# First attention's squares as rounded high and low parts, and two later norm sums one feature tile earlier

## The chip, the core and the metric

The kernel runs on one core of a Trainium2 chip. The metric is the device time of one execution in microseconds (us), as the median of several runs. TensorE (PE) multiplies matrices into PSUM; VectorE (DVE), ScalarE (ACT) and GpSimd (POOL) do the elementwise work; SyncE (SP) issues nearly all loads. Each engine has a queue of its own that it works through in order; they meet only at semaphores.

## The reference, cut to what matters

Two transformer blocks run one after the other on a sequence of 512 positions of width 1024, in float32. The first block has a sliding-window attention whose queries (8 heads of 64) and keys (2 heads of 64) are normalised head by head:

```python
def rmsnorm(x, gain):
    xf = x.astype(jnp.float32)
    y = xf * lax.rsqrt(jnp.mean(xf * xf, axis=-1, keepdims=True) + NORM_EPS)
    return (y * gain.astype(jnp.float32)).astype(x.dtype)
...
    q = rmsnorm(q.reshape(B, S, N_Q_HEADS, HEAD_DIM), q_gain)
    k = rmsnorm(k.reshape(B, S, N_KV_HEADS, HEAD_DIM), k_gain)
...
        x = x + merged @ w_out[l]
        x = x + conv_gated_mlp(rmsnorm(x, ffn_norm[l]), w_up[l], conv_w[l], conv_b[l], w_down[l])
```

The means over 64 features are the sums that the first part of the change makes in another way. The second part moves the sums of two norms over the whole width of 1024: the one ahead of the gated MLP (called norm 2 in the kernel) and the one with which the second block begins (norm 3).

## The kernel before

Features lie on the 128 partitions and positions along the free dimension, so a projection is a set of products of a 128x128 weight tile with a 128x512 activation tile. To keep float32 accuracy each operand is split in a rounded high part and the rounded rest (type fp32r), and three passes are made for each feature tile: high by high, high by low, low by high (lines 394 to 396). The weights come in strips of 128x1024, loaded by SP. For each strip n DVE makes `w_high` (`make_high`, line 368) and POOL makes `w_low` (`make_low`, line 373). A strip's two parts live in rings of four (`w_high`, `w_low`), the raw strip in a ring of two (`w_raw`), so the load of strip n + 2 waits for `make_low` of strip n, and `make_high` of strip n + 4 waits until PE has used strip n.

The part that matters here is the projection of keys, values and queries, strips 8 to 13 (`N_QKV` + m, m = 0 to 5): keys m = 0, values m = 1, queries m = 2 to 5. PE runs the six strips in turn, cut in two pieces each from m = 1 on (`cuts`), and puts small work between the pieces. Between the pieces of strip m = 2 to 5 stands `qkv_sum(m - 2)`, and `qkv_sum(4)` follows after the first of four small mixing products (`mix(0)`, line 1017). The five sums j = 0 to 4 belong to the keys and the four query strips. For each j the chain is:

- ACT squares the finished projection out of PSUM into `sq` (line 1757).
- PE multiplies `sq` by the constant `blocks`, which holds ones in two 64x64 blocks, so that each partition gets its head's sum (`qkv_sum`, line 955). Both are plain float32, and the profile has two PE instructions for one such product.
- ACT takes Ln and Exp (lines 1747 and 1750), DVE multiplies the projection by the result (`i1_norm`, line 2292).

ACT does them in turn: squares j, Ln j, Exp j, squares j + 1. DVE has other work between the norms, in a fixed order: norm 0, `make_high` of strips 12 and 13, a copy of the values, two `bias_h` tables (line 2298); norm 1, `make_high` 14; norm 2, two copies of turned tokens, `make_high` 15; norm 3, two copies (line 2305), `make_high` 16; the first mixing result (lines 2327 and 2330), norm 4. POOL only makes `w_low` of strips 12 to 17 in this stretch. After `mix(1)` PE waits for the last Exp and starts the attention scores (`a_scores`, line 1031).

Norm 2 works so: while the output projection ends, ACT writes squares of each new feature tile and POOL adds the first seven up in `root`. PE starts the MLP's up projection on the raw tiles, before they are normalised (`product_two`, lines 407 to 411, six passes for a feature tile, since two strips go together), and stops after three feature tiles to sum over the partitions (`norm_rest`, lines 498 and 500, again plain float32). ACT takes the root, DVE scales (line 529), ACT rounds, DVE makes the low part (line 533), tile by tile; PE's product with strip m = 2 needs these tiles one by one. Norm 3 has the same form ahead of the second block's projections.

Of the kernel before, what the change touches and what calls it, by code (L numbers as in the profile page):

```python
# [7 lines left out]
ACT = mybir.ActivationFunctionType  # L8
ALU = mybir.AluOpType
AX = mybir.AxisListType  # L10
F32 = mybir.dt.float32
# [4 lines left out]
KT = D // P  # L16
S = 512
# [65 lines left out]
def program(nc, x, mix_norm, w_in, q_norm, k_norm, sinks, sgu_norm, w_s, b_s, w_oa, w_ob, w_out,  # L83
# [4 lines left out]
    with ExitStack() as ctx:  # L88
# [24 lines left out]
        sq = sb("sq", [P, 2, L])  # L113
# [111 lines left out]
        ps = ctx.enter_context(nc.psum_tensor("ps", [P, 8, 512], F32))  # L225
# [144 lines left out]
        def make_low(pool, n, i=0):  # L370

            pool.wait_ge(high_made, i + (n + 1))
            pool.tensor_tensor(w_low[:, n % RING, :], w_raw[:, n % RAW, :],  # L373
                               w_high[:, n % RING, :].bitcast(F32), ALU.subtract).then_inc(low_made, 1)
# [24 lines left out]
        def product_two(pe, banks, n, high, low, done, ks=(0, KT), used=None, moving=None):  # L399

            for k in range(*ks):
                mh, ml = (moving or hx)(k)
                at = slice(k * P, (k + 1) * P)
                pe.wait_ge(s[high], done + k + 1)
                for o in range(2):
                    slot = (n + o) % RING
                    pe.matmul(ps[:, banks[o], :], w_high[:, slot, at], mh, start=k == 0, stop=False)  # L407
                    pe.matmul(ps[:, banks[o], :], w_low[:, slot, at], mh, start=False, stop=False)  # L408
                pe.wait_ge(s[low], done + k + 1)
                for o in range(2):  # L410
                    mm = pe.matmul(ps[:, banks[o], :], w_high[:, (n + o) % RING, at], ml, start=False, stop=k == KT - 1)  # L411
                    if k == KT - 1:
                        mm.then_inc(strip_used, 1)
                if used and k < KT - 1:
                    mm.then_inc(s[used], 1)
# [22 lines left out]
        def yx(k):  # L438
# [5 lines left out]
            norm_sq norm_sum norm_added norm_root norm_scaled norm_high norm_low  # L444
            gelu_done sv_sq sv_sum sv_root sv_normed sv_turned sv_tok_ready mixed mix_biased mix_gated
            mix_high
            i1_sq i1_sum i1_ln i1_root i1_normed v_made
            j_staged j_bias a_scored a_masked a_neg a_part a_exp a_sink_exp a_probs a_turned
            a_copied a_summed a_y a_high a_low gate_kept
            g_sig m_part m_whole m_high_ m_low_ o_added  # L450
# [198 lines left out]
        def _(pool):  # L649
# [14 lines left out]
            pool.wait_ge(s["more_in"], 16 * N_EARLY)  # L664
            for dst, src in more[N_EARLY:]:
                pool.dma_start(dst, src).then_inc(s["more_in"], 16)
            for n in range(2, N_GATE):
                make_low(pool, n)
                if n in (9, 10):
                    pool.wait_ge(s["sv_sq"], n - 7)  # L670
                    if n == 10:
                        pool.wait_ge(s["sv_sum"], 1)
                    pool.tensor_tensor(root[:, 1, 0:S], sq[:, 0, 0:S], sq[:, 1, 0:S] if n == 9 else root[:, 1, 0:S],
                                       ALU.add).then_inc(s["sv_sum"], 1)
                if n == 3:

                    pool.wait_ge(s["meta_in"], 16)
                    pool.affine_select(out=ws_raw[:], in_=ws_raw[:], compare_op=ALU.is_ge, fill=0.0, base=0,
                                       pattern=[[0, 8], [-1, P]], channel_multiplier=1).then_inc(s["ws_made"], 1)
            for n0, n1 in ((N_GATE, N_MERGE), (N_MERGE, N_OUT)):  # L680
                with pool.Fori(0, (n1 - n0) // 4) as turn:
                    i = turn * 4
                    for n in range(n0, n0 + 4):
                        make_low(pool, n, i)
# [181 lines left out]
        def _(pe):  # L866
# [82 lines left out]
            bank = [4, 5, 6, 7, 4, 5]  # L949

            def qkv_sum(j):
                pe.wait_ge(s["i1_sq"], j + 1)
                if j >= 2:
                    pe.wait_ge(s["i1_root"], j - 1)
                pe.matmul(ps[:, j % 2, :], blocks[:], sq[:, j % 2, 0:S], start=True, stop=True)\
                    .then_inc(s["i1_sum"], 1)


# [125 lines left out]
            mix(0)  # L1084
            qkv_sum(4)
            mix(1)
            pe.wait_ge(s["i1_root"], 5)
            a_scores(0, 0, first=True)
            mix(2)
            mix(3)  # L1090
# [31 lines left out]
            def raw(k):  # L1122
                return m_high[:, FT - KT + k, :], m_low[:, FT - KT + k, :]

            product_two(pe, (0, 1), N_UP, "raw_high", "raw_low", 0, (0, 3), moving=raw)
            norm_rest(pe, 2, ps[:, 7, :])
            product_two(pe, (0, 1), N_UP, "raw_high", "raw_low", 0, (3, KT), moving=raw)
            for m in range(2, 4):
                pe.wait_ge(low_made, N_UP + m + 1)
                pe.wait_ge(s["o_added"], 8)  # L1130
# [18 lines left out]
                            part == 0, part == 2, ready=("z_low", 8 * part) if m == 0 else None)\  # L1149
                        .then_inc(strip_used, 1)  # L1150
            pe.wait_ge(low_made, N_LAT + 2)
            product_two(pe, (0, 1), N_LAT, "raw_high", "raw_low", KT, (0, 3), "raw_used")
            norm_rest(pe, 3, ps[:, 6, :])
            product_two(pe, (0, 1), N_LAT, "raw_high", "raw_low", KT, (3, KT), "raw_used")

            def kv_rows(m, k0, k1):
                pe.wait_ge(low_made, N_LAT + m + 1)
# [520 lines left out]
        def _(act):  # L1678
# [62 lines left out]
            def i1_root(j):  # L1741
                act.wait_ge(s["i1_sum"], j + 1)
                if j >= 2:
                    act.wait_ge(s["i1_normed"], j - 1)
                if j == 1:
                    act.wait_ge(s["sv_normed"], 4)
                act.activation(root[:, j % 2, 0:S], ps[:, j % 2, :], ACT.Ln, bias=eps[:, 0:1], scale=1.0 / HD)\
                    .then_inc(s["i1_ln"], 1)
                act.wait_ge(s["i1_ln"], j + 1)
                act.activation(root[:, j % 2, 0:S], root[:, j % 2, 0:S], ACT.Exp, scale=-0.5)\  # L1750
                    .then_inc(s["i1_root"], 1)

            for j in range(5):
                act.wait_ge(strip_used, N_QKV + strips[j] + 1)
                if j >= 2:
                    act.wait_ge(s["i1_sum"], j - 1)
                act.activation(sq[:, j % 2, 0:S], ps[:, banks[j], :], ACT.Square).then_inc(s["i1_sq"], 1)
                if j == 0:
                    act.wait_ge(strip_used, N_QKV + 2)
                    act.activation(v_f[:], ps[:, 5, :], ACT.Copy).then_inc(s["v_made"], 1)  # L1760
                if j < 4:
                    i1_root(j)
# [39 lines left out]
            a_pair(3, more=False)  # L1802


            act.activation(blocks_r[:], blocks[:], ACT.Copy)
            act.activation(ones_r[:], ones[:], ACT.Copy)
            after(act, "att")
            with act.Fori(0, 2) as i:
# [422 lines left out]
        def _(dve):  # L2231
# [54 lines left out]
            dve.wait_ge(s["more_in"], 16 * N_MORE)  # L2286

            def i1_norm(j):
                dve.wait_ge(s["i1_root"], j + 1)
                dst = k_t[:] if j == 0 else q_t[:, j - 1, :]  # L2290
                gain = col(V_AK) if j == 0 else aq_gain[:, 0:1]
                dve.scalar_tensor_tensor(dst, ps[:, [4, 6, 7, 4, 5][j], :], gain, root[:, j % 2, 0:S],
                                         ALU.mult, ALU.mult).then_inc(s["i1_normed"], 1)
# [673 lines left out]
```

## Time and profile before

| | us |
|---|---|
| median of 3 runs | 1268.66 |
| lowest and highest run | 1268.24, 1270.27 |
| the profiled execution | 1269.92 |
| its span in the trace | 1268.2 |
| PE busy with matmuls | 1246.8 |
| DVE busy | 720.4 |
| POOL busy | 637.5 |
| ACT busy | 467.8 |

The span reaches from the first to the last instruction in the trace; the profiled execution's own time is 1.7 us longer. The busy times overlap: an engine that has less to do than PE still matters where PE waits for it. Line numbers are those of the kernel before, where nothing else is said.

### The profile page before, as it was taken

How to read it: one execution, taken by the hardware profiler on the slowest of the kernel's cores; microseconds unless marked ns; L12 is line 12 of the kernel's file. 1: busy time of each engine (PE TensorE's matmuls, PEld its weight loads, DVE VectorE, ACT ScalarE, POOL GpSimd, SP SyncE). 2: the span in 40 equal slices, each digit the busy share in tenths (PEclk: the TensorE clock that was granted, in tenths of full speed). 3: DMA queues.
4: the chain of work that ended last, by engine and by line, in shares of the span. 5: the costliest groups of instructions: out<-in, count | busy, mean ns of one | idle time of the engine just before them, and what ended most of it. 6: DMA issues, size and time to landing. Idle time of an engine off the chain costs nothing.

```text
span 1268.2 us, 19971 instructions
## 1 busy us (share of the span) xinstructions
PE 1246.8 (98%) x6772; PEld 1031.6 (81%) x6772; DVE 720.4 (57%) x1380; ACT 467.8 (37%) x1019; POOL 637.5 (50%) x426
## 2 busy tenths in 40 slices
PE   7999999999999999999999999999999999999998
PEld 6877777877788888888887878988988888888876
DVE  5236655566865545452223788888744566666640
ACT  4233333412322222221112476776511445555531
POOL 5443333237353444445664154544537877777722
PEclk9999999999999999999999999999999999999999
DMA  7322222223233333323334211211134333322113
GB/s 206 101 67 67 83 83 67 68 83 101 87 111 99 92 90 91 107 79 92 91 97 124 67 51 40 59 36 38 55 82 112 92 86 81 83 79 79 66 34 100
DMA packets 190612, 105.42 MB, mean 83 GB/s; under 512 B 19175, under 2 KB 186445, under 8 KB 190557
## 3 DMA queue, kind: packets, MB, share of 16 engines
q1 hardware_dynamic: 189748, 102.82, 28.7%
q10 hardware_dynamic: 376, 1.18, 0.2%
q0 software_dynamic: 432, 0.69, 0.2%
q8 instruction: 33, 0.54, 0.2%
q14 instruction: 23, 0.18, 0.0%
HBM read 102.57 MB, written 2.10 MB: 83 GB/s over the span
## 4 chain that ended last, share of the span: by engine, by line
PE 87%; DVE 4%; ACT 3%; issue 2%; POOL 2%; DMA 1%; ACTq 0%; DVEq 0%; SPq 0%; POOLq 0%
PE ps L394 20%; PE ps L395 19%; PE ps L396 19%; PE ps L425 8%; PE ps L1572 1%; PE ps L1574 1%; PE ps L1573 1%; PE ps L1230 1%; PE ps L1489 1%; PE ps L1521 1%; POOL w_low L373 1%; PE ps L1501 1%; PE ps L407 1%; PE ps L408 1%; PE ps L411 1%
## 5 line engine op out<-in xcount | busy, mean ns | idle before, releaser
L373 POOL TENSOR_TENSOR w_low<-w_raw,w_high 128x1024 fp32r<-128x1024 f32 x180 | 440.6, 2450 | 435.5 <-DVE w_high L368 430.3
L394 PE MATMUL ps<-h_high,w_high 128*128 128x512 f32 x810 | 325.7, 402 | 0.5 <-DVE h_low L533 0.4
L395 PE MATMUL ps<-h_low,w_high 128*128 128x512 f32 x810 | 320.2, 395 | 0.0
L396 PE MATMUL ps<-h_high,w_low 128*128 128x512 f32 x810 | 318.8, 394 | 0.0
L368 DVE CAST w_high<-w_raw 128x1024 fp32r<-128x1024 f32 x183 | 144.0, 789 | 116.9 <-DMA w_raw<-in_w_in_dram 39.4
L394 PEld LDWEIGHTS ps<-h_high,w_high 128*128 128x128 f32 x810 | 152.2, 188 | 36.0 <-issue 2.3
L396 PEld LDWEIGHTS ps<-h_high,w_low 128*128 128x128 f32 x810 | 152.4, 188 | 34.7
L395 PEld LDWEIGHTS ps<-h_low,w_high 128*128 128x128 f32 x810 | 152.2, 188 | 32.2 <-issue 1.0
L1839 ACT ACTIVATE z<-ps,cv 128x512 f32<-128x512 f32 x42 | 32.7, 778 | 148.3 <-PE ps L396 148.3
L2470 DVE SCALAR_TENSOR_TENSOR z<-ps,cv,z 128x511 f32<-128x511 f32 x42 | 31.5, 749 | 92.9 <-ACT z L1839 92.8
L396 PE MATMUL ps<-m_high,w_low 128*128 128x512 f32 x176 | 69.4, 395 | 0.0
L395 PE MATMUL ps<-m_low,w_high 128*128 128x512 f32 x176 | 69.4, 395 | 0.0
L394 PE MATMUL ps<-m_high,w_high 128*128 128x512 f32 x176 | 69.4, 394 | 0.0
L425 PE MATMUL ps<-h_high,w_high 128*128 128x264 f32 x304 | 65.1, 295 | 0.0
L425 PE MATMUL ps<-h_high,w_low 128*128 128x264 f32 x304 | 61.8, 285 | 0.0
L425 PE MATMUL ps<-h_low,w_high 128*128 128x264 f32 x304 | 61.7, 284 | 0.0
L792 POOL TENSOR_TENSOR nb<-rel,mask 128x128 f32<-128x128 f32 (+1 forms) x96 | 53.4, 595 | 0.3 <-DMA rel<-in_rel_bias_dram 0.3
L2778 DVE TENSOR_SCALAR ne<-ne,nm 128x272 f32<-128x272 f32 (+2 forms) x64 | 51.3, 842 | 1.1
L425 PEld LDWEIGHTS ps<-h_high,w_high 128*128 128x128 f32 x304 | 47.8, 189 | 3.9 <-issue 2.8
L425 PEld LDWEIGHTS ps<-h_low,w_high 128*128 128x128 f32 x304 | 47.1, 188 | 0.0
L425 PEld LDWEIGHTS ps<-h_high,w_low 128*128 128x128 f32 x304 | 47.0, 188 | 0.0
L1858 ACT ACTIVATE x_t<-z 128x512 f32<-128x512 f32 x8 | 9.8, 1224 | 100.5 <-DVE z L2498 100.5
(406 smaller groups left out, 2424.4 us busy)
## 6 DMA issues: line engine op xcount, KB each, us to landing
w_raw<-in_w_in_dram SPq DMA_DIRECT2D x150, 256.0 KB, 3.2
w_raw<-in_w_up_dram SPq DMA_DIRECT2D x88, 256.0 KB, 3.2
w_raw<-in_w_out_dram SPq DMA_DIRECT2D x44, 256.0 KB, 3.0
w_raw<-in_w_down_dram SPq DMA_DIRECT2D x32, 256.0 KB, 3.0
w_raw<-in_w_down_dram SPq DMA_DIRECT2D x16, 192.0 KB, 2.6
rel<-in_rel_bias_dram SPq DMA_DIRECT2D x16, 192.0 KB, 3.7
w_raw<-in_w_ob_dram SPq DMA_DIRECT2D x8, 256.0 KB, 3.0
w_raw<-in_w_oa_dram SPq DMA_DIRECT2D x8, 256.0 KB, 4.1
```

The costliest lines, as they stand in the source:

```text
L368: dve.tensor_copy(w_high[:, n % RING, :], w_raw[:, n % RAW, :]).then_inc(high_made, 1)
L373: pool.tensor_tensor(w_low[:, n % RING, :], w_raw[:, n % RAW, :], w_high[:, n % RING, :].bitcast(F32), ALU.subtract).then_inc(low_made, 1)
L394: pe.matmul(acc, wh, mh, start=first and k == 0, stop=False)
L395: pe.matmul(acc, wh, ml, start=False, stop=False)
L396: done = pe.matmul(acc, wl, mh, start=False, stop=last and k == tiles - 1)
L407: pe.matmul(ps[:, banks[o], :], w_high[:, slot, at], mh, start=k == 0, stop=False)
L408: pe.matmul(ps[:, banks[o], :], w_low[:, slot, at], mh, start=False, stop=False)
L425: done = pe.matmul(ps[:, bank + h, 0:HALF], wt, mt[:, k, h * HALF:h * HALF + HALF], start=one_, stop=end)
L792: pool.tensor_tensor(to, half_tiles(rel[:, h, :], r, n), half_tiles(mask[:], m, n), ALU.add)\
L1839: act.activation(z[:, m, :], src, ACT.Identity, scale=cv[:, bass.ds(i * 2 + (C_CONV + 2 * 2 * FT + ct), 1)], bias=cv[:, bass.ds(i * 2 + (C ...
L2470: dve.scalar_tensor_tensor(z[:, m, 1:S], src[:, 0:S - 1], cv[:, bass.ds(i * 2 + (C_CONV + 2 * FT + ct), 1)], z[:, m, 1:S], ALU.mult, ALU.a ...
L2778: p = dve.tensor_scalar(ne[:, t % 2, h, 0:w], ne[:, t % 2, h, 0:w], nm[:, t % 2, 2, h:h + 1], None, ALU.mult)
```

## The change

Three things are changed in the first attention's sums. ACT writes each square twice, in float32 into `sq` and rounded into `a_high` (two tiles of a buffer that the attention fills only later). POOL makes the rest, `sq` minus `a_high`, into `a_low` (`i1_square_low`). PE sums the two parts in two rounded passes with a rounded `blocks_r`, for which the copy is moved from behind the attention to ahead of the first square. The wait of the sum is now for POOL's part. The semaphore `i1_ln` is gone; its steps are counted in `i1_root`, and PE's wait for the sum's PSUM bank is now for the Ln that reads it, no longer for the Exp behind it. And the two `norm_rest` stand behind two feature tiles instead of three.

```diff
             for n in range(2, N_GATE):
+                if n == N_QKV + 4:
+                    i1_square_low(0)
                 make_low(pool, n)
...
+            def i1_square_low(j):
+
+                pool.wait_ge(s["i1_sq"], 2 * j + 2)
+                pool.tensor_tensor(a_low[:, j % 2, :], sq[:, j % 2, 0:S], a_high[:, j % 2, :].bitcast(F32),
+                                   ALU.subtract).then_inc(s["i1_sq_low"], 1)
...
+            for j in range(1, 5):
+                i1_square_low(j)
+                make_low(pool, N_GATE + j - 1)
...
             def qkv_sum(j):
-                pe.wait_ge(s["i1_sq"], j + 1)
+                pe.wait_ge(s["i1_sq_low"], j + 1)
                 if j >= 2:
-                    pe.wait_ge(s["i1_root"], j - 1)
-                pe.matmul(ps[:, j % 2, :], blocks[:], sq[:, j % 2, 0:S], start=True, stop=True)\
+                    pe.wait_ge(s["i1_root"], 2 * j - 3)
+                pe.matmul(ps[:, j % 2, :], blocks_r[:], a_high[:, j % 2, :], start=True, stop=False)
+                pe.matmul(ps[:, j % 2, :], blocks_r[:], a_low[:, j % 2, :], start=False, stop=True)\
                     .then_inc(s["i1_sum"], 1)
...
-            product_two(pe, (0, 1), N_UP, "raw_high", "raw_low", 0, (0, 3), moving=raw)
+            product_two(pe, (0, 1), N_UP, "raw_high", "raw_low", 0, (0, 2), moving=raw)
             norm_rest(pe, 2, ps[:, 7, :])
...
+            act.wait_ge(s["more_in"], 16 * N_MORE)
+            act.activation(blocks_r[:], blocks[:], ACT.Copy)
             for j in range(5):
...
                 act.activation(sq[:, j % 2, 0:S], ps[:, banks[j], :], ACT.Square).then_inc(s["i1_sq"], 1)
+                act.activation(a_high[:, j % 2, :], ps[:, banks[j], :], ACT.Square).then_inc(s["i1_sq"], 1)
...
-            act.activation(blocks_r[:], blocks[:], ACT.Copy)
             act.activation(ones_r[:], ones[:], ACT.Copy)
```

On POOL, from the adds of the gating norm's squares to the end of the stretch, the order before is this (the three strips in one row are 11, 12 and 13; the loop behind makes 14 to 29):

```order
L673 TENSOR_TENSOR root<-sq 128x512
L373 TENSOR_TENSOR w_low<-w_raw,w_high 128x1024
L673 TENSOR_TENSOR root<-sq,root 128x512
L373 TENSOR_TENSOR w_low<-w_raw,w_high 128x1024 x3
L681 UNCONDITIONAL_BRANCH
```

And this is POOL's order in the changed kernel at the same place (line 670 is the new subtraction):

```order
L373 TENSOR_TENSOR w_low<-w_raw,w_high 128x1024
L670 TENSOR_TENSOR a_low<-sq,a_high 128x512
L373 TENSOR_TENSOR w_low<-w_raw,w_high 128x1024 x2
L670 TENSOR_TENSOR a_low<-sq,a_high 128x512
L373 TENSOR_TENSOR w_low<-w_raw,w_high 128x1024
L670 TENSOR_TENSOR a_low<-sq,a_high 128x512
L373 TENSOR_TENSOR w_low<-w_raw,w_high 128x1024
L670 TENSOR_TENSOR a_low<-sq,a_high 128x512
L373 TENSOR_TENSOR w_low<-w_raw,w_high 128x1024
L670 TENSOR_TENSOR a_low<-sq,a_high 128x512
L373 TENSOR_TENSOR w_low<-w_raw,w_high 128x1024
L692 UNCONDITIONAL_BRANCH
```

The subtraction for j = 0 stands ahead of strips 12 and 13, that for j = 1 behind both, and those for j = 2, 3 and 4 each behind the strip 14, 15 and 16.

On PE, at the fifth sum between the first two mixing products, the kernel before has these rows, with the semaphores that each waits for:

```order
L396 MATMUL ps<-h_high,w_low 128x512
L1017 MATMUL ps<-ws_t,uv_tok 64x128 [waits sv_tok_ready]
L1017 MATMUL ps<-ws_t,uv_tok 64x128 x7
L955 MATMUL ps<-sq,blocks 128x512 [waits i1_root,i1_sq]
L1017 MATMUL ps<-ws_t,uv_tok 64x128 [waits sv_tok_ready]
L1017 MATMUL ps<-ws_t,uv_tok 64x128 x7
L1031 MATMUL ps<-k_t,q_st 128x128 [waits j_staged,i1_root]
```

And the changed kernel has these, where line 1029 is the mixing product and line 1043 the scores:

```order
L396 MATMUL ps<-h_high,w_low 128x512
L1029 MATMUL ps<-ws_t,uv_tok 64x128 [waits sv_tok_ready]
L1029 MATMUL ps<-ws_t,uv_tok 64x128 x7
L966 MATMUL ps<-a_high,blocks_r 128x512 [waits i1_root,i1_sq_low]
L967 MATMUL ps<-a_low,blocks_r 128x512
L1029 MATMUL ps<-ws_t,uv_tok 64x128 [waits sv_tok_ready]
L1029 MATMUL ps<-ws_t,uv_tok 64x128 x7
L1043 MATMUL ps<-k_t,q_st 128x128 [waits j_staged,i1_root]
```

The places of the sums among PE's other work are the same; what the sum waits for and the number of its instructions differ.

## Rows read from the trace of the kernel before

**Rows 1.** The page, part 1: busy time, share of the span, instructions.
```profile
PE 1246.8 (98%) x6772; PEld 1031.6 (81%) x6772; DVE 720.4 (57%) x1380; ACT 467.8 (37%) x1019; POOL 637.5 (50%) x426
```

**Rows 2.** PE's waits over the whole span: us in total, times, longest us.
```profile
PE ps L871 <- DMA ident<-in_c_ident_dram: 4.7, 1, 4.7
PE ps L1501 <- DVE ne L2778: 1.4, 2, 1.1
```

**Rows 3.** Timeline around the fourth sum: start us, us, engine, line, operation, count.
```profile
102.80 0.39 PE L396 MATMUL ps<-h_high,w_low 128*128 128x512 f32 x1
...
103.03 1.02 PE L955 MATMUL ps<-sq,blocks 128*128 128x512 f32 x2
...
104.12 0.39 PE L395 MATMUL ps<-h_low,w_high 128*128 128x512 f32 x1
```

**Rows 4.** A subtraction of 128x512 on POOL, line 731: ns min/median/max.
```profile
L731 POOL TENSOR_TENSOR qn_low<-q_f,qn_high x8: 1287/1290/1299, 735.9 to 902.6; 128x512 fp32r<-128x512 f32 x8
```

**Rows 5.** Timelines of single engines around the second sum.
```profile
84.93 1.29 DVE L368 CAST w_high<-w_raw 128x1024 fp32r<-128x1024 f32 x2
...
85.69 5.17 POOL L373 TENSOR_TENSOR w_low<-w_raw,w_high 128x1024 fp32r<-128x1024 f32 x2 [10.40 <-DVE w_high L368]
...
85.40 0.60 ACT L1757 ACTIVATE sq<-ps 128x512 f32<-128x512 f32 x1 [1.17 <-PE ps L396]
89.06 0.69 ACT L1747 ACTIVATE root<-ps,eps 128x512 f32<-128x512 f32 x1 [3.06 <-PE ps L955]
...
88.00 1.02 PE L955 MATMUL ps<-sq,blocks 128*128 128x512 f32 x2
```

**Rows 6.** Timelines of PE and POOL around the third and fourth sum.
```profile
95.30 1.02 PE L955 MATMUL ps<-sq,blocks 128*128 128x512 f32 x2
...
93.26 2.39 POOL L373 TENSOR_TENSOR w_low<-w_raw,w_high 128x1024 fp32r<-128x1024 f32 x1 [2.40 <-DVE w_high L368]
100.37 2.39 POOL L373 TENSOR_TENSOR w_low<-w_raw,w_high 128x1024 fp32r<-128x1024 f32 x1 [4.71 <-DVE w_high L368]
```

**Rows 7.** Timeline from the first mixing product to the scores, all engines.
```profile
107.48 1.09 PE L1017 MATMUL ps<-ws_t,uv_tok 128*64 128x128 f32 x16 [0.65 <-DVE uv_tok L2305]
108.10 2.36 POOL L373 TENSOR_TENSOR w_low<-w_raw,w_high 128x1024 fp32r<-128x1024 f32 x1 [5.34 <-DVE w_high L368]
...
108.50 1.12 PE L955 MATMUL ps<-sq,blocks 128*128 128x512 f32 x2
...
109.34 1.66 DVE L2330 TENSOR_TENSOR uv<-uv,scaled 128x512 f32<-128x512 f32 x1
...
111.06 0.93 PE L1031 MATMUL ps<-k_t,q_st 64*128 64x128 f32 x8 [0.41 <-ACT root L1750]
```

**Rows 8.** Timelines at norm 2: PE, POOL and DVE.
```profile
319.75 1.02 PE L498 MATMUL ps<-root,ones 128*128 128x512 f32 x2
...
328.46 0.40 PE L394 MATMUL ps<-h_high,w_high 128*128 128x512 f32 x1
...
335.17 0.40 PE L394 MATMUL ps<-h_high,w_high 128*128 128x512 f32 x1
...
320.25 2.37 POOL L373 TENSOR_TENSOR w_low<-w_raw,w_high 128x1024 fp32r<-128x1024 f32 x1 [1.26 <-DVE w_high L368]
...
323.06 1.42 DVE L529 SCALAR_TENSOR_TENSOR scaled<-x_t,cv,root 128x512 f32<-128x512 f32 x2 [2.88 <-ACT root L518]
```

**Rows 9.** Timelines at norm 3: PE, ACT and DVE.
```profile
690.00 1.02 PE L498 MATMUL ps<-root,ones 128*128 128x512 f32 x2
...
688.75 0.62 ACT L512 ACTIVATE sq<-x_t 128x512 f32<-128x512 f32 x1
...
698.85 1.29 DVE L2523 TENSOR_TENSOR mg<-ps,root 128x512 f32<-128x512 f32 x2 [0.63 <-PE ps L411]
```

**Rows 10.** PE's timeline at the program's start, two groups of sixteen transposes.
```profile
6.12 3.68 PE L875 MATMUL ps<-ident,x_tok 128*128 128x128 f32 x16 [1.14 <-DMA x_tok<-in_x_dram]
...
20.36 1.91 PE L875 MATMUL ps<-ident,x_tok 128*128 128x128 f32 x16
```

More of the change, by code:

```diff
@@ L446, in program @@
             mix_high
-            i1_sq i1_sum i1_ln i1_root i1_normed v_made
+            i1_sq i1_sq_low i1_sum i1_root i1_normed v_made
             j_staged j_bias a_scored a_masked a_neg a_part a_exp a_sink_exp a_probs a_turned
@@ L679, in _ @@
                                        pattern=[[0, 8], [-1, P]], channel_multiplier=1).then_inc(s["ws_made"], 1)
-            for n0, n1 in ((N_GATE, N_MERGE), (N_MERGE, N_OUT)):
-                with pool.Fori(0, (n1 - n0) // 4) as turn:
+            for j in range(1, 5):
+                i1_square_low(j)
+                make_low(pool, N_GATE + j - 1)
+            for n0, n1, t0 in ((N_GATE, N_MERGE, 1), (N_MERGE, N_OUT, 0)):
+                with pool.Fori(t0, (n1 - n0) // 4) as turn:
                     i = turn * 4
@@ L1086, in _ @@
             mix(1)
-            pe.wait_ge(s["i1_root"], 5)
+            pe.wait_ge(s["i1_root"], 10)
             a_scores(0, 0, first=True)
@@ L1123, in raw @@
                 return m_high[:, FT - KT + k, :], m_low[:, FT - KT + k, :]
-            product_two(pe, (0, 1), N_UP, "raw_high", "raw_low", 0, (0, 3), moving=raw)
+            product_two(pe, (0, 1), N_UP, "raw_high", "raw_low", 0, (0, 2), moving=raw)
             norm_rest(pe, 2, ps[:, 7, :])
-            product_two(pe, (0, 1), N_UP, "raw_high", "raw_low", 0, (3, KT), moving=raw)
+            product_two(pe, (0, 1), N_UP, "raw_high", "raw_low", 0, (2, KT), moving=raw)
             for m in range(2, 4):
@@ L1151, in _ @@
             pe.wait_ge(low_made, N_LAT + 2)
-            product_two(pe, (0, 1), N_LAT, "raw_high", "raw_low", KT, (0, 3), "raw_used")
+            product_two(pe, (0, 1), N_LAT, "raw_high", "raw_low", KT, (0, 2), "raw_used")
             norm_rest(pe, 3, ps[:, 6, :])
-            product_two(pe, (0, 1), N_LAT, "raw_high", "raw_low", KT, (3, KT), "raw_used")
+            product_two(pe, (0, 1), N_LAT, "raw_high", "raw_low", KT, (2, KT), "raw_used")
             def kv_rows(m, k0, k1):
@@ L1747, in i1_root @@
                 act.activation(root[:, j % 2, 0:S], ps[:, j % 2, :], ACT.Ln, bias=eps[:, 0:1], scale=1.0 / HD)\
-                    .then_inc(s["i1_ln"], 1)
-                act.wait_ge(s["i1_ln"], j + 1)
+                    .then_inc(s["i1_root"], 1)
+                act.wait_ge(s["i1_root"], 2 * j + 1)
                 act.activation(root[:, j % 2, 0:S], root[:, j % 2, 0:S], ACT.Exp, scale=-0.5)\
                     .then_inc(s["i1_root"], 1)
+            act.wait_ge(s["more_in"], 16 * N_MORE)
+            act.activation(blocks_r[:], blocks[:], ACT.Copy)
             for j in range(5):
@@ L2288, in i1_norm @@
             def i1_norm(j):
-                dve.wait_ge(s["i1_root"], j + 1)
+                dve.wait_ge(s["i1_root"], 2 * j + 2)
                 dst = k_t[:] if j == 0 else q_t[:, j - 1, :]
```

## The prediction

> **What bounds the kernel now.** I read the page's busy times first. PE is busy for 1246.8 of 1268.2 us [rows 1]. The table of PE's waits comes next: the longest wait is the one for the first data, 4.7 us, and the longest wait after the first microseconds is 1.1 us [rows 2]. So the kernel is bound by PE nearly everywhere, and two things can move the time: what PE itself runs, and new waits of PE. A new wait of 1 us is paid in full, because no large idle time of PE stands behind it in which it could be made good. After that I read the timelines around the five sums and the two norms, engine by engine, since this is where the change adds a step between two engines.
>
> **What the sums save on PE.** In rows 3 a strip's last pass starts at 102.80 and the sum at 103.03, so a rounded pass costs 0.23 us of PE. The sum's two float32 instructions and one strip pass end where the next one starts, at 104.12: 1.09 us, less 0.23 for the strip pass, is 0.86 for the sum. Two rounded passes cost 0.47. The change saves 0.39 us for each sum, 1.95 us for five, if the sum finds its operands ready.
>
> **What it adds.** ACT gets five more squares of 0.60 us [rows 5] and one copy earlier. ACT sits idle for 1.17 us before the second square and 3.06 us behind it [rows 5], so the new square alone is hidden there. POOL gets five subtractions of 128x512 at 1.29 us [rows 4]. POOL has idle time enough (10.40 us before strip 12) [rows 5], but its queue is in order, and the question is what stands ahead of each subtraction. I go through them.
>
> Sum 0: its square is the first of the stretch, POOL idles before strip 12 for 10.40 us, and the subtraction stands ahead of that strip. No wait. PE gains 0.39, and all that hangs on the sum comes 0.39 earlier.
>
> Sum 1: the subtraction stands behind `w_low` of strips 12 and 13, both. Their cause is sum 0 itself: DVE casts these strips only after norm 0. They run from 85.69 to 90.86 [rows 5], and 0.39 earlier in the changed kernel, to 90.47. Adding 1.29 gives 91.76, and with some 0.05 for the semaphore the sum starts at 91.8. PE reaches it at 88.00 - 0.39 = 87.6 [rows 5]. **PE waits for 4.2 us.** ACT's two squares end at 85.40 - 0.39 + 1.2 = 86.2, long before, so POOL's order is what decides.
>
> Sum 2: the cast of strip 14 follows norm 1, and that follows sum 1 at 91.8. In the kernel before, POOL starts strip 15 at 100.37, 5.07 us behind sum 2 [rows 6]: Ln, Exp, norm, two copies, cast. For strip 14 the two copies are missing, which I put at a cast's 0.64 each [rows 5], and the sum itself is 0.39 shorter: 5.07 - 1.28 - 0.39 = 3.4. `w_low` of strip 14 starts at 95.2 and takes 2.39 [rows 6], the subtraction ends at 98.9, and sum 2 starts at 98.95. PE reaches it 3.4 us later than before (4.2 of wait less two savings), at 95.30 + 3.4 = 98.7 [rows 6]. Wait 0.25, and behind the sum PE is 3.3 us late.
>
> Sum 3: `w_low` of strip 15 now starts 5.07 - 0.39 behind 98.95, at 103.65, ends at 106.0, and the subtraction at 107.3. PE reaches the sum at 103.03 + 3.3 = 106.3 [rows 3]. Wait 1.0; behind the sum PE is 3.9 us late.
>
> Sum 4: `w_low` of strip 16 started 5.07 us behind sum 3 as well (103.03 to 108.10) [rows 3, 7]. It now starts at 107.35 + 4.68 = 112.0, ends at 114.4, and the subtraction at 115.65. PE starts the first mixing product at 107.48 + 3.9 = 111.4 and reaches the sum at 108.50 + 3.9 = 112.4 [rows 7]. **Wait 3.3 us.** The scores followed sum 4 by 2.56 us [rows 7], since PE waited for the Exp; now by 2.17. They start at 115.7 + 2.17 = 117.9 instead of 111.06: PE is 6.8 us late.
>
> One thing may come on top. DVE's product of 109.34 took 1.66 us and ended 0.54 us behind POOL's work of 108.10 to 110.46 [rows 7]: it sat there until POOL was done. It is waiting again when POOL goes from strip 16 to the subtraction. If it slips between, the subtraction ends up to 0.55 later; if not, nothing is lost. I take 0.2. The Trainium skill, "SBUF — State Buffer", section "Who interferes with whom", says that these two engines' shared port pair is held for a whole instruction and that the other engine blocks; the trace agrees with its 1.66 us. By that rule the price is one whole instruction or none, never a share of one, so the sum would be 6.8 or 7.35.
>
> Behind the scores the chain to the first turned probabilities starts from the scores, and shifts with PE; the strips' low parts are made earlier relative to PE. I expect no wait to go and none to come there. First part: **+7.0 us**, the savings included (bounds 5.5 and 7.7: the lower one if POOL's strips are each some 0.3 us shorter than the rows say and less of each wait is left).
>
> **What the earlier norm sums bring.** A raw feature tile costs PE six passes, 1.40 us; its work stays the same, only the sum is made 1.40 earlier. At norm 2 PE uses the normalised tiles one by one and is held up: a strip of 24 passes takes 6.71 us from 328.46 to 335.17 [rows 8] where 24 x 0.23 is 5.5, so 1.2 us is the most to be had. DVE would be released at 323.06 - 1.40 = 321.66, but POOL works on a strip from 320.25 to 322.62 [rows 8], and DVE's scaling reads two SBUF tiles, as the product of 109.34 did. As there, it would end 0.54 behind POOL, at 323.16, instead of about 323.77 (half of 1.42 behind 323.06). That is 0.6 gained; I take -0.6, with 0 and -1.2 as bounds. At norm 3 the last square ends at 689.37 [rows 9]. The sum's second half, which needs it, is reached at 690.00 - 1.40 + 0.43 = 689.0 at the soonest, or 0.86 behind 688.60 if the two float32 instructions of the first half count in full, which they do: 689.46. No wait. But halfway through its tiles DVE stands idle for 0.63 us for PE's last raw pass and goes on at 698.85 [rows 9], whenever the sum was made. What was won ahead of that point is lost there. Norm 3: 0, between +0.1 and -0.3. The rounded copy moved away from behind the attention, on an ACT that waits there, is 0.
>
> **The sum.** +7.0 - 0.6 + 0 = +6.4 us. Against the profiled execution's 1269.92 (span 1268.2 and 1.7 around it) this is 1276.3; that execution lies 1.3 us above the median of 1268.66, and against the median it is 1275.1. I forecast 1275.1 us.
>
> **Rivals.**
> 1. *The sums are covered, and faster.* If POOL's part reached every sum in time, the change would be what its passes say: -1.95 - 0.6 = -2.55, or 1266.1. For it speaks that POOL is idle half the time [rows 1]. Against it stands POOL's order: the two strips ahead of the second subtraction end at 90.86 and their cast is released by the first sum. It could hold only if the two 4 us and 3 us waits were made good elsewhere, and rows 2 show no idle time to do so.
> 2. *Only the second sum's wait counts.* If the fifth sum were not held up (the subtraction ready ahead of strip 16), PE would be late by 3.9 - 0.39 and win 0.6: +2.9, or 1271.6. Against it: PE's square for the fifth sum comes at about the time of strip 16's cast, and that strip stands first in POOL's queue.
> 3. *PE slows down after the long wait.* No wait over 1.1 us occurs inside the program, so the trace does not show what PE does after 4 us of idleness. The nearest rows are the program's start: after the wait of 4.7 us the first sixteen transposes took 3.68 us and sixteen like them later 1.91 [rows 2, 10], 1.8 us more. If this happened after one wait it would be +1.8 for a stretch like that and up to 3.5 for one twice as long; after both, up to 7. One gives 1276.9 to 1278.6. The Trainium skill, "TensorE: Matmul & The Clock Gate", section "HAM oscillation — how this bites in real kernels", holds that an idle gap that is long enough sends TensorE back to the lower of its two clock levels, 1.2 instead of 2.4 GHz; the page of the profile shows the granted clock at its full level throughout, so no run here shows it yet. By that rule a wait like that of sum 1 is the one at risk.
> 4. *Against the norm part.* The sum is made before its last square and PE waits: at norm 3 the square (689.37) and the moment at which it is needed (689.46) lie within 0.1. This is worth 0.1 at most and stands in the range.
>
> **How the numbers follow.** Forecast (both long waits, no slower clock) 0.70. Slower clock on top 0.14. Only the second sum's wait 0.06. Covered and faster 0.06. What is left, 0.04, I give to something that I have not seen that makes no difference. About 0.2% (2.5 us) is what a measurement of this kernel can tell from no change. Forecast, clock case and the second rival at +2.9 all lie over it: slower 0.89. Same 0.05, faster 0.06, this last only just, since -2.55 is at the bound. The forecast's own range is 5.5 - 1.5 to 7.7 + 0.1, +4.0 to +7.8: 1272.7 to 1276.5. To this I add 0.5 us below for the spread of the runs (their lowest is 0.42 under the median) and reach above into the clock case for one stretch: **1272.2 to 1279.0**, which leaves out the two smaller rivals and the doubled clock case, some 0.16 in all.
>
> **What the profile of the changed kernel would show.** The table of PE's waits should get a wait for POOL's `a_low` at the sums: five uses, about 9 us in total, the longest about 4.2 us. The timeline should have the second sum at about 91.8 and the scores at about 117.9. Each sum takes 0.47 us of PE. At norm 2 the strip behind the raw tiles should need about 6.1 us instead of 6.71. If the granted clock falls below its full level near 92 or 116 us, the third rival holds. I am wrong if POOL's subtraction for j = 1 ends before 88 us, or if a wait elsewhere in the program shrinks by microseconds.

## The result and the profile after

The changed kernel takes 1279.47 us (median of 4 runs, 1278.24 to 1281.21), the kernel before 1269.42 us (4 runs, 1268.24 to 1270.27). The ratio is 1.0082 with a 95% interval of 1.0069 to 1.0094: **slower by some 10 us**. The forecast had the sign and the mechanism, 1275.1 us, but not the size: the measured time lies 0.5 us above its range of 1272.2 to 1279.0. The forecast was added to 1268.66, the median of three runs of the kernel before; a fourth run of it, 1270.18, brought that median to 1269.42.

The table of PE's waits, over the whole span (us in total, times, longest us), is the first view to read against [rows 2]:

```profile
PE ps L966 <- POOL a_low L670: 8.4, 3, 4.0
...
PE ps L1513 <- DVE ne L2792: 0.2, 1, 0.2
```

There is a new first row: three of the five head sums wait for POOL's subtraction, 8.4 us together. PE's wait for DVE's tile `ne` was 1.4 us in [rows 2]; here it is 0.2. PE's busy time in the page did not fall, though the sums' passes got cheaper (1246.8 us in [rows 1]):

```profile
PE 1247.5 (98%) x6772; PEld 1032.9 (81%) x6772; DVE 718.0 (56%) x1380; ACT 471.4 (37%) x1024; POOL 644.6 (50%) x431
```

The timeline of POOL answers to [rows 5 to 7] (start us, us, engine, line, operation, count, and what ended the idle time before):

```profile
85.36 5.12 POOL L373 TENSOR_TENSOR w_low<-w_raw,w_high 128x1024 fp32r<-128x1024 f32 x2 [6.27 <-DVE w_high L368]
90.45 1.31 POOL L670 TENSOR_TENSOR a_low<-sq,a_high 128x512 fp32r<-128x512 f32 x1
95.88 2.39 POOL L373 TENSOR_TENSOR w_low<-w_raw,w_high 128x1024 fp32r<-128x1024 f32 x1 [4.13 <-DVE w_high L368]
98.23 1.29 POOL L670 TENSOR_TENSOR a_low<-sq,a_high 128x512 fp32r<-128x512 f32 x1
...
113.42 2.35 POOL L373 TENSOR_TENSOR w_low<-w_raw,w_high 128x1024 fp32r<-128x1024 f32 x1 [4.84 <-DVE w_high L368]
115.72 1.71 POOL L670 TENSOR_TENSOR a_low<-sq,a_high 128x512 fp32r<-128x512 f32 x1
```

Each of the last four subtractions runs straight behind a strip. The fifth took 1.71 us instead of 1.3. PE's timeline over the same stretch, with its waits:

```profile
81.88 0.39 PE L966 MATMUL ps<-a_high,blocks_r 128*128 128x512 f32 x1
...
91.81 0.80 PE L966 MATMUL ps<-a_high,blocks_r 128*128 128x512 f32 x1 [3.98 <-POOL a_low L670]
92.40 0.63 PE L967 MATMUL ps<-a_low,blocks_r 128*128 128x512 f32 x1
92.83 0.63 PE L394 MATMUL ps<-h_high,w_high 128*128 128x512 f32 x1
93.25 0.63 PE L395 MATMUL ps<-h_low,w_high 128*128 128x512 f32 x1
...
95.21 0.40 PE L394 MATMUL ps<-h_high,w_high 128*128 128x512 f32 x1
...
117.49 0.79 PE L966 MATMUL ps<-a_high,blocks_r 128*128 128x512 f32 x1 [3.60 <-POOL a_low L670]
118.08 0.63 PE L967 MATMUL ps<-a_low,blocks_r 128*128 128x512 f32 x1
...
120.55 1.65 PE L1043 MATMUL ps<-k_t,q_st 64*128 64x128 f32 x8
...
124.08 0.50 PE L394 MATMUL ps<-h_high,w_high 128*128 128x512 f32 x1
```

The second sum starts at 91.81, where the forecast put it at 91.8. But look at the starts behind it: 92.83, 93.25, the passes come every 0.43 us, and from 95.21 on every 0.23 us again. The scores took 1.65 us where they had taken 0.93 [rows 7]. The stretches of the span with the granted clock (length; PE busy; PEclk; DMA) say why:

```profile
88.00:91.80 3.80, 0.00 (x0) 0.97 0.50 140
91.80:95.30 3.50, 3.49 (x9) 0.55 0.49 147
95.30:100.00 4.70, 4.70 (x26) 1.00 0.04 9
...
113.90:117.40 3.50, 0.00 (x0) 0.72 0.06 16
117.40:122.60 5.20, 5.11 (x34) 0.53 0.32 93
122.60:126.00 3.40, 3.40 (x38) 1.00 0.00 0
```

In both long waits TensorE's granted clock goes to half, 1.2 instead of 2.4 GHz, and PE starts again at the lower level. The two falls don't come at the same point of their waits. In finer slices the clock falls at about 91.6 us in the first one, 3.7 us after PE ran out of work at 87.83. In the second one it falls at about 115.5 us, only 1.6 us after PE ran out of work at 113.89.

For all kernels below I measure the attention stretch by itself, from the start of the first head sum to the first pass of the gate strips (line 394 behind the scores). The first head sum starts at 81.57 to 83.18 us in the ten profiles, though PE has the same instructions ahead of it in all of them, and this spread is left out so. Before it is 32.00 us (the sum at 81.82, the gate pass at 113.82), after it is 124.08 - 81.88 = 42.20: **+10.2 us**.

### The profile page after: what moved, and what is told of

The parts are those of the page before. It is cut to its first block, busy times and chain, and to the rows that moved or that the text cites. A ratio compares the mean times of both kernels' runs of the same rounds, so it can differ in the third digit from the quotient of the medians.

```text
span 1276.5 us, 19975 instructions
## 1 busy us (share of the span) xinstructions
PE 1247.5 (98%) x6772; PEld 1032.9 (81%) x6772; DVE 718.0 (56%) x1380; ACT 471.4 (37%) x1024; POOL 644.6 (50%) x431
## 4 chain that ended last, share of the span: by engine, by line
PE 88%; DVE 4%; POOL 3%; ACT 2%; issue 2%; DMA 1%; ACTq 0%; DVEq 0%; SPq 0%; POOLq 0%
PE ps L394 20%; PE ps L395 19%; PE ps L396 19%; PE ps L425 8%; POOL w_low L373 2%; PE ps L1584 1%; PE ps L1586 1%; PE ps L1585 1%; PE ps L1501 1%; PE ps L1533 1%; PE ps L1242 1%; PE ps L1513 1%; PE ps L407 1%; PE ps L1043 1%; PE ps L408 1%
## 5 line engine op out<-in xcount | busy, mean ns | idle before, releaser
L2792 DVE TENSOR_SCALAR ne<-ne,nm 128x272 f32<-128x272 f32 (+2 forms) x64 | 45.5, 751 | 1.1
```

The source lines that it names most:

```text
L2792: p = dve.tensor_scalar(ne[:, t % 2, h, 0:w], ne[:, t % 2, h, 0:w], nm[:, t % 2, 2, h:h + 1], None, ALU.mult)
```

## The experiments

My theory is that three things add up: PE's waits for subtractions that stand behind strips in POOL's queue, the lower clock that follows the two long ones, and a small gain from the norms. The rivals are that the added work itself costs (on ACT, on POOL, or by blocking DVE), that the norm part is to blame, and that split sums are too long a chain whatever the order.

**The added work without the wait** (`plain_sum_added_work`). All that ACT and POOL have more to do stays, in its place. Only the sum is as before.

```diff
-                pe.wait_ge(s["i1_sq_low"], j + 1)
+                pe.wait_ge(s["i1_sq"], 2 * j + 1)
...
-                pe.matmul(ps[:, j % 2, :], blocks_r[:], a_high[:, j % 2, :], start=True, stop=False)
-                pe.matmul(ps[:, j % 2, :], blocks_r[:], a_low[:, j % 2, :], start=False, stop=True)\
+                pe.matmul(ps[:, j % 2, :], blocks[:], sq[:, j % 2, 0:S], start=True, stop=True)\
```

ACT waits for the subtraction two sums back before it writes over its operands. The norm part of the change is kept.

> The changed kernel with all that it adds on ACT and POOL kept (second square, copy, subtraction in the same places), but PE sums the float32 square with the float32 blocks again and waits only for that square, not for POOL. It gives the same values as before. My theory (PE's wait for POOL's place in the queue is the cause, not the added work): no wait over 1.1 us, clock at full level, time within 1 us of before. Rival (added work on ACT and POOL, or its blocking of DVE at the shared tiles, delays the chain): +2 us or more.

Measured: 1268.05 us against 1269.36, ratio 0.9992 (0.9982 to 1.0001). The profile's stretch is 32.00 us, to the hundredth that of before:

```profile
82.97 1.02 PE L966 MATMUL ps<-sq,blocks 128*128 128x512 f32 x2
...
114.97 0.50 PE L394 MATMUL ps<-h_high,w_high 128*128 128x512 f32 x1
```

Five more squares, five subtractions and the earlier copy cost nothing as long as PE doesn't wait for them. The added work does hold DVE up: in the changed kernel two gating products at 77.85 us took 2.45 us beside the first subtraction, where they had taken 1.41, and a copy of two columns at 90.55 took 1.22 instead of 0.16 beside the second. No wait of PE comes from either. The whole loss hangs on PE's wait for the subtractions.

I had expected the clock at its full level, and in the attention it was. But it was low from about 13.6 to 17.0 us, far ahead of the attention, behind a wait of PE of 2.13 us for ACT. This is part of why the first sum starts late in this profile, at 82.97. At the same place, waits of 2.82 us in `filled`, 2.17 in `last_plain` and 2.14 in `norms_only` left the clock full.

**The norms alone** (`norms_only`). The kernel before with the tile ranges (0, 2) and (2, KT) at both norms.

```diff
-            product_two(pe, (0, 1), N_UP, "raw_high", "raw_low", 0, (0, 3), moving=raw)
+            product_two(pe, (0, 1), N_UP, "raw_high", "raw_low", 0, (0, 2), moving=raw)
             norm_rest(pe, 2, ps[:, 7, :])
-            product_two(pe, (0, 1), N_UP, "raw_high", "raw_low", 0, (3, KT), moving=raw)
+            product_two(pe, (0, 1), N_UP, "raw_high", "raw_low", 0, (2, KT), moving=raw)
```

> The kernel before with only the two norm sums moved behind two feature tiles. My theory (the norm part gains little because POOL's strip and PE's last raw pass hold DVE): PE wins 0.6 us at the strip behind norm 2 and loses 0.1 to 0.2 at norm 3, together 0.4 to 0.5 us, about 0.9996 of before, not to be told from no change. Rival (DVE's whole chain moves 1.40 us): 1.1 us at norm 2 and more at norm 3, 0.999 or less. Rival (the earlier sums cost a wait): slower.

Measured: 1268.05 against 1269.36 us, 0.9991 (0.9982 to 1.0000), which time alone hardly tells from no change, and which would fit the rival (0.999) as well as my 0.9996. The profile decides: from the first gate pass to the first wide pass behind norm 3 (line 425) it took 584.83 us before (113.82 to 698.65) and 584.34 here (114.05 to 698.39), 0.5 us less, and in the changed kernel 584.42 (124.08 to 708.50). All ten profiles fall in these two groups: 584.80 and 584.83 in the two with the old place of the sums, 584.32 to 584.48 in the eight with the new one. At norm 3 the sum does come too early by a little. In the changed kernel's timelines of ACT and PE:

```profile
698.46 0.62 ACT L512 ACTIVATE sq<-x_t 128x512 f32<-128x512 f32 x1
...
698.30 1.02 PE L498 MATMUL ps<-root,ones 128*128 128x512 f32 x2
699.22 1.10 PE L500 MATMUL ps<-sq,ones 128*128 128x512 f32 x2
```

The second half starts 0.92 us behind the first where it took 0.86 before. The last square ends at 699.08, 0.14 us ahead of it, which is the likely reason. And the DVE timeline shows what the forecast said would swallow the rest at norm 3, a wait for PE's last raw pass, now 1.32 us instead of the 0.63 of [rows 9]:

```profile
708.70 1.29 DVE L2537 TENSOR_TENSOR mg<-ps,root 128x512 f32<-128x512 f32 x2 [1.32 <-PE ps L411]
```

**The sums alone** (`sums_only`). The changed kernel with both norm sums behind three tiles again (the diff above, turned round).

> The changed kernel with both norm sums back behind three tiles, so the five head sums' change alone. My theory: all of the 10 us and about 0.5 more are here, +10 to +11 us, 1.0083; second and fifth sum wait 4.0 and 3.6 us for POOL and the granted clock falls to half behind each. Rival (the norm part or something far from the attention is the cause): clearly under +8 us.

Measured: 1280.11 against 1269.36 us, 1.0093 (1.0079 to 1.0107). All of the loss is in the five head sums. The stretch is 43.96 us in this profile (81.74 to 125.70), 1.8 more than in the changed kernel, and the clock was low for a longer piece behind the second sum, which makes 1.1 of the 1.8:

```profile
86.00:90.40 4.40, 1.68 (x8) 1.00 0.22 59
90.40:97.00 6.60, 5.35 (x13) 0.51 0.41 119
```

So the clock's part varies from execution to execution. Here it was low up to 97.3 us, in the changed kernel's profile only up to 95.0. The other 0.7 us stands behind the scores, where the clock was low up to 124.6 us, 1.1 us ahead of the gate strips; in the changed kernel it was full again from 122.3 on, 1.8 us ahead of them. The four timed runs of the changed kernel fit that: mean clocks of 0.996, 0.996, 0.995 and 0.994 go with spans of 1276.5, 1277.0, 1278.5 and 1279.5 us. They don't prove it, since the spans of the kernel before vary by 3 us and more with hardly any difference in the mean clock.

**The waits filled with work** (`filled`). To tell the wait from the clock, PE runs strip passes while it waits. They go into the sum's own bank, and the sum overwrites them.

```diff
+                if j in (1, 4):
+                    if j == 4:
+                        pe.wait_ge(s["i1_root"], 5)
+                    for _ in range(17 if j == 1 else 15):
+                        pe.matmul(ps[:, j % 2, :], w_high[:, (N_QKV + 5) % RING if j == 4 else (N_QKV + 3) % RING, 0:P],
+                                  h_high[:, 0, META:L], start=True, stop=True)
                 pe.wait_ge(s["i1_sq_low"], j + 1)
```

> The changed kernel with idle waiting turned into idle work: 17 strip passes ahead of the second head sum and 15 ahead of the fifth, written into the sum's own PSUM bank, whose content the sum then overwrites, so nothing is computed with them. They take 17 x 0.233 = 4.0 and 3.5 us, as long as the waits of 4.0 and 3.6. My theory (the waits cost about 7 us and a lower clock behind them another 3.2, 1.55 behind the second sum and 1.66 behind the fifth): the granted clock stays at its full level and the time falls by about 3 us against the changed kernel, to +7 us against before. Rival (the clock record is a bystander and the excess has another cause): the time stays at +10.

Measured: 1277.39 against 1269.36 us, 1.0068 (1.0053 to 1.0084). PE's timeline and the clock by stretches:

```profile
82.35 0.39 PE L972 MATMUL ps<-a_high,blocks_r 128*128 128x512 f32 x1
...
88.13 4.12 PE L967 MATMUL ps<-h_high,w_high 128*128 128x512 f32 x17
92.37 0.50 PE L972 MATMUL ps<-a_high,blocks_r 128*128 128x512 f32 x1
...
119.21 0.93 PE L1049 MATMUL ps<-k_t,q_st 64*128 64x128 f32 x8 [0.42 <-ACT root L1768]
...
121.97 0.50 PE L394 MATMUL ps<-h_high,w_high 128*128 128x512 f32 x1
```

```profile
92.00:96.00 4.00, 3.89 (x19) 1.00 0.45 131
...
118.00:123.00 5.00, 4.58 (x61) 1.00 0.12 37
```

The clock stays at its full level, the scores take 0.93 us again, and the stretch is 39.62 us, 2.6 under the changed kernel's 42.20, where I expected about 3. The waits less the saved passes cost 7.6 us, and the clock 2.6 in this pair of profiles. Adding useless passes made the stretch shorter; the medians differ by 2.1 us the same way, but the intervals of the two ratios overlap from 1.0069 to 1.0084, so the whole kernel's time shows it less surely than the stretch.

**Only the second wait filled** (`filled_second`). The same with `if j == 1` and 17 passes.

> The changed kernel with 17 strip passes into the sum's own PSUM bank ahead of the second head sum only, overwritten by the sum. My theory: the granted clock keeps its full level behind the second sum and still falls near the fifth; the time lies 1.0 to 1.5 us under the changed kernel, about +8.7 against before. Rival (the clock falls for another reason than PE's idleness before it): it falls in both places as before.

Measured: 1277.85 against 1268.54 us, 1.0070 (1.0055 to 1.0086), +9.3 us by the medians. The stretch is 41.11 us (83.18 to 124.29): 1.1 under the changed kernel. In its timeline the passes behind the second sum run at full speed and the scores are slow again (1.62 us):

```profile
117.78 0.80 PE L970 MATMUL ps<-a_high,blocks_r 128*128 128x512 f32 x1 [3.60 <-POOL a_low L670]
...
120.84 1.62 PE L1047 MATMUL ps<-k_t,q_st 64*128 64x128 f32 x8
```

The clock's fall depends on PE being idle, place by place: filling the second sum's wait wins 1.1 us, filling the fifth's too another 1.5.

**The second subtraction moved ahead** (`second_first`). POOL makes it before strips 12 and 13; the others stay behind their strips.

```diff
                 if n == N_QKV + 4:
                     i1_square_low(0)
+                    i1_square_low(1)
                 make_low(pool, n)
...
             for j in range(1, 5):
-                i1_square_low(j)
+                if j >= 2:
+                    i1_square_low(j)
                 make_low(pool, N_GATE + j - 1)
```

> The changed kernel with POOL's subtraction for the second sum moved ahead of the low parts of strips 12 and 13; all else in its order, so the third, fourth and fifth subtraction still stand behind strips 14, 15 and 16. My theory (every sum is tied to the sum before it through DVE's cast and POOL's strip): the second sum's wait of 4 us goes, to start near 87.6, but the third sum then waits 3.8 us in its place, since strip 14 still comes between (landing of its load near 94, low part to 97, subtraction to 98.2), so only 0.6 us is won: about +9.5 us against before, clock falling twice again. Rival (the two long waits are independent costs): 4 us of wait and 1.5 us of clock are won, +4.5 to +5 us against before.

Measured: 1277.10 against 1268.54 us, 1.0067 (1.0051 to 1.0082), +8.6 us by the medians where I expected +9.5.

```profile
81.57 0.39 PE L968 MATMUL ps<-a_high,blocks_r 128*128 128x512 f32 x1
87.36 0.40 PE L968 MATMUL ps<-a_high,blocks_r 128*128 128x512 f32 x1
97.95 0.50 PE L968 MATMUL ps<-a_high,blocks_r 128*128 128x512 f32 x1 [3.51 <-POOL a_low L670]
106.40 0.51 PE L968 MATMUL ps<-a_high,blocks_r 128*128 128x512 f32 x1 [0.86 <-POOL a_low L670]
...
115.26 0.79 PE L968 MATMUL ps<-a_high,blocks_r 128*128 128x512 f32 x1 [3.60 <-POOL a_low L670]
```

The second sum's wait is gone, and the third has one of 3.51 us instead, because strip 14 stands ahead of its subtraction. The total of the waits went from 8.4 to 8.0 us. So far this is as expected. But what frees strip 14 here is not the start of a sum, as in my theory. In DVE's and POOL's timelines of this run:

```profile
93.57 0.69 DVE L368 CAST w_high<-w_raw 128x1024 fp32r<-128x1024 f32 x1 [0.87 <-DMA w_raw<-in_w_in_dram]
94.34 2.34 POOL L373 TENSOR_TENSOR w_low<-w_raw,w_high 128x1024 fp32r<-128x1024 f32 x1 [2.32 <-DVE w_high L368]
```

The cast of strip 14 waited last for its load, which was issued at 89.80, when POOL was done with strip 12. Strip 12 started on POOL only at 87.16, behind the moved subtraction, instead of 85.36 in the changed kernel. So it is again POOL's order that makes the third wait, but by way of the raw strips' ring. From the third sum on the chain is the one of the theory: the fourth sum starts 8.45 us behind the third and the fifth 8.86 behind the fourth, against 8.36 and 8.85 in the changed kernel. One thing I had not expected: the stretch is 40.25 us, 2.0 less than the changed kernel's, though only 0.4 us of waiting went. Most of the rest is the clock. It fell in the wait of the fifth sum but not in this one of 3.51 us:

```profile
94.00:98.00 4.00, 0.49 (x3) 1.00 0.37 109
98.00:102.00 4.00, 3.88 (x18) 1.00 0.45 131
...
115.00:120.00 5.00, 4.74 (x28) 0.50 0.35 101
```

**Every subtraction ahead of its strips** (`all_first`). The second as above, and the loop behind it in the other order, so that subtraction j = 2, 3, 4 stands ahead of strip 14, 15, 16.

```diff
-            for j in range(1, 5):
+            for j in range(2, 5):
                 i1_square_low(j)
-                make_low(pool, N_GATE + j - 1)
+                make_low(pool, N_GATE + j - 2)
+            make_low(pool, N_GATE + 3)
```

> The changed kernel with each subtraction ahead of the strips that stand in front of it: the second ahead of 12 and 13, the third ahead of 14, the fourth ahead of 15, the fifth ahead of 16. Same work on every engine. My theory (only POOL's order makes the loss): second sum near 87.6, third near 94.5, fourth near 101.8 without waits, the fifth waits 0.8 us for the second square and the subtraction behind the last query strip; clock at its full level; 1 us won at the scores and 0.45 at the norms, -1.0 to -1.7 us against before, 0.9990. Rival (the split sums are too long a chain wherever POOL makes them): still slower than before.

Measured: 1267.68 against 1268.54 us, 0.9991 (0.9982 to 1.0000), -0.9 us by the medians. The same instructions on every engine as in the changed kernel, and by the two ratios some 11 us faster. PE's timeline:

```profile
87.97 0.41 PE L968 MATMUL ps<-a_high,blocks_r 128*128 128x512 f32 x1
94.90 0.40 PE L968 MATMUL ps<-a_high,blocks_r 128*128 128x512 f32 x1
102.24 0.40 PE L968 MATMUL ps<-a_high,blocks_r 128*128 128x512 f32 x1
...
108.17 0.50 PE L968 MATMUL ps<-a_high,blocks_r 128*128 128x512 f32 x1 [0.78 <-POOL a_low L670]
```

The second to fourth sum wait for nothing, the fifth for 0.78 us (forecast 0.8). The stretch is 30.90 us (82.19 to 113.09), 1.1 less than before. Split sums are not too long a chain, then, if POOL makes their parts in time.

**The fifth sum in plain float32** (`last_plain`). As `all_first`, but for j = 4 there is no rounded square and no subtraction, and PE sums the float32 square.

```diff
+                if j == 4:
+                    pe.matmul(ps[:, 0, :], blocks[:], sq[:, 0, 0:S], start=True, stop=True).then_inc(s["i1_sum"], 1)
+                    return
```

> As all_first, but the fifth sum is made in plain float32 from the float32 square, with neither rounded square nor subtraction, since its chain is short of time. My theory: the four split sums bring 4 x 0.39 = 1.56 us, the fifth no longer waits, the norms bring 0.45: -2.0 us against before, 0.9984, and 0.5 us faster than all_first. Rival (PE's saved passes are lost again at the waits for the turned tokens and for the last Exp): within 0.5 us of before.

Measured: 1267.59 against 1268.54 us, 0.9991 (0.9982 to 1.0001). The stretch is 30.45 us (82.08 to 112.53), 1.55 less than before, where four times 0.39 is 1.56. The medians show 0.95 us of the 2.0 that I expected. Timing does not separate it from `all_first`, nor for certain from the kernel before; the stretches of single profiles differ by 0.45 and 1.55 us.

## Why the forecast was right and where it was wrong

Intervals between PE's milestones show the steps of the forecast one by one (us; `filled` has the waits without the lower clock):

| from, to | before | forecast | `filled` | changed |
|---|---|---|---|---|
| sum 1, sum 2 | 6.18 | 9.98 | 10.02 | 9.93 |
| sum 2, sum 3 | 7.30 | 7.15 | 7.27 | 8.47 |
| sum 3, sum 4 | 7.73 | 8.40 | 8.46 | 8.36 |
| sum 4, sum 5 | 5.47 | 8.35 | 8.94 | 8.85 |
| sum 5, scores | 2.56 | 2.17 | 2.17 | 3.06 |
| scores, gate pass | 2.76 | 2.76 | 2.76 | 3.53 |

**POOL's queue as the cause: right, and shown.** Added work without the wait costs 0.00 us, the same work with all subtractions ahead of their strips turns +10.2 us into -1.1 in the stretch. The wait of the second sum was to be 4.2 us and was 3.98 (4.14 counted from starts of passes, as the forecast did), the fifth's 3.3 (3.5 with DVE's product) and 3.60.

**DVE's product between strip and subtraction: right in kind, undersized.** The forecast gave it 0.2 of a possible 0.55. The subtraction took 1.71 us instead of 1.27 to 1.31 for its neighbours without a waiting DVE, 0.42 us more. It slipped in in all six profiles in which the fifth subtraction follows strip 16 on POOL (1.71 to 1.74 us). In `all_first`, where it precedes strip 16, it took 1.27. So the whole 0.4 should have stood in the sum. The Trainium skill's rule in "SBUF — State Buffer", section "Who interferes with whom", of a pair of ports that one engine holds for a whole instruction fits this and the 1.65 us of the product; the price here was 0.42 us, less than the 0.69 that such a product takes alone. In the table it is most of the 0.6 us that sum 4 to sum 5 has over the forecast.

**The clock: the step that failed.** The forecast named a lower clock as the third rival with a chance of 0.14, and priced it for one wait at 1.8 to 3.5 us. Its sum of +6.4 holds nothing for it, and its range reaches only to one such stretch. It happened in both waits, and at 1.1 to 1.5 us each it was cheaper than the price. Against `filled` it costs 1.2 us from sum 2 to sum 3, 0.9 from sum 5 to the scores and 0.8 behind them, 2.9 together, less 0.3, since three other intervals are 0.1 us longer each in `filled`. The stretch loses 2.6 us by it in the changed kernel's profile and 1.8 more in that of `sums_only`. The error was in the odds and in the price, not in the mechanism: the forecast had two waits of over 3 us in a program in which no wait of that length occurred behind the start, and took the missing evidence for a small chance. The price came from [rows 10], which are poor evidence: the sixteen transposes there take twice as long as later, but the view gives the granted clock as 1.00 in that stretch, so it does not tell whether the clock was the reason. The rule of the Trainium skill that it cited, "TensorE: Matmul & The Clock Gate", section "HAM oscillation — how this bites in real kernels", says that an idle gap that is long enough brings the lower level; the traces of the changed kernel agree, in both places. But the length of a wait alone did not tell: the clock stayed full through the 3.51 us in `second_first`, while it fell 1.6 us into the wait of the fifth sum here.

**The passes' saving: right.** 0.39 us a sum: sum 5 to the scores is 2.17 in `filled`, and four saved sums bring 1.55 us in `last_plain`.

**The norms: right.** -0.6 was forecast as the sum of both, and 0.4 to 0.5 us is measured. At norm 2 the strip behind the raw tiles was to need about 6.1 us instead of 6.71, and it took 6.13 (338.72 to 344.85). Its longest wait is now 0.20 us, where it was 0.42:

```profile
338.72 0.39 PE L394 MATMUL ps<-h_high,w_high 128*128 128x512 f32 x1
...
343.26 0.50 PE L394 MATMUL ps<-h_high,w_high 128*128 128x512 f32 x1 [0.20 <-DVE h_low L533]
...
344.85 0.40 PE L394 MATMUL ps<-h_high,w_high 128*128 128x512 f32 x1
```

At norm 3 nothing was won and about 0.1 lost, as the bound had it.

**Summed up.** +7.6 for the waits less the savings, +2.6 for the clock, -0.4 for the norms is +9.8 us, where the medians differ by 10.0. The profiled spans differ by only 8.3 (1276.5 against 1268.2), because the profile of the kernel before holds 1.2 us more of the wait for `ne` than the one after, 1.4 in [rows 2] against 0.2; `filled_second` and `plain_sum_added_work` have it again (1.3 and 1.4) and the other experiments have 0.2 or less, so it seems to belong to an execution and not to the change. Some 0.3 us of the difference I can't place.

Against the forecast's 1275.1 us the measured 1279.47 is 4.4 more. Of this, 2.6 us are the clock, 0.6 the waits (7.6 against 7.0), 0.2 the norms (0.4 against 0.6), 0.8 the median before, which was 0.76 higher with the fourth run, and 0.2 stay open.

Rival 1 (covered and faster) describes what `all_first` does with the same work: it is the order of one queue that decides between it and the forecast. Rival 2, that the fifth sum is not held up, fell with the 3.60 us wait.

## What to carry to other kernels

When a step is handed to an engine that is idle half the time, read what stands ahead of it in that engine's queue and what frees that; if the thing ahead is itself freed by the result of the new step, a wait can arise at every turn. Removing it in one place only may move it to the next, as it did here. Put the short step that PE waits for ahead of the long ones that nobody needs yet. And where a new wait keeps PE idle for as long as the waits here (six of 3.60 to 3.98 us, all six with a fall of the clock), count a lower clock as likely, here 1 to 1.5 us for each and at times more, until a profile says otherwise.

## What the runs showed of the hardware

In four profiles (`after`, `sums_only`, `filled_second`, `second_first`) PE had six idle waits of 3.60 to 3.98 us at the second or fifth sum. In all six the granted clock fell, and passes behind the second sum came every 0.43 us instead of 0.23. In one wait of 3.51 us in `second_first` it did not fall. The length of a wait alone does not tell: within these six, the clock fell 1.3 to 3.7 us after PE had run out of work, and near the program's start it fell behind a wait of 2.13 us in one profile and stayed full behind 2.14 to 2.82 us in three others. How long it stayed low varied too, to 95.0 us in the changed kernel and to 97.3 in `sums_only` behind the same wait. Passes whose results nobody reads kept the clock up and made the stretch 2.6 us shorter. A product on DVE that waited behind POOL's strip ran between that strip and the subtraction behind it, which took 1.71 instead of 1.29 us for it. And a float32 product with 512 columns takes PE 0.86 us as two instructions, against 0.23 for a rounded pass, so a pair of rounded passes is worth 0.39 us, if the low part comes for nothing.
